# Down projections of three feed-forward layers: two narrow matmuls merged into one of 512 columns, eight PSUM banks in use, and the low halves added to x a chunk earlier

## The chip, the cores and the metric

The kernel runs on one core of a Trainium2 chip, as one program. The metric is the device time of one execution in microseconds (us). The median of three runs of the kernel before is 1074.24 us (1074.14 to 1075.94).

## The reference

Two transformer blocks over 256 tokens of width 1024, batch 1. The first has MoBA attention and differential attention, a cross attention to 256 memory tokens, a SwiGLU feed-forward layer and a final norm. The second is two layers deep: an attention and convolution mixer, then a gated linear attention mixer, each with a convolutional feed-forward layer and a per-layer embedding. Three parts of it hold the change, the down projections at the end of the three feed-forward layers. In the reference they are the last product of

```
def swiglu(x, norm_g, w_gate, w_up, w_down):
    h = rms_norm(x, norm_g)
    return (jax.nn.silu(h @ w_gate) * (h @ w_up)) @ w_down
...
        x = x + swiglu(x, ffn_norm_g[l], w_gate[l], w_up[l], w_down[l])
```

and the same in `_conv_ffn` of the second block, with a depthwise convolution and GELU ahead of it. The hidden width is 2816, the output width 1024, all in float32.

## The kernel before, in words

Activations lie features first: a tile has 128 features on the partitions and 256 tokens (T) in the free dimension; x has 8 such tiles (KT). A float32 product is made of three fp32r matmuls. Each operand is split into a high part (the fp32r rounding) and a low part (the rest): high weight times high activation, high weight times low activation, low weight times high activation, all summed in PSUM.

Weights come in chunks of 128 x 2048 (1 MB), one DMA each, through three slots (U) of `raw`. ScalarE (ACT) writes the high part of a chunk to `w_hi`, VectorE (DVE) the low part to `w_lo`, both two chunks ahead of the chunk that TensorE (PE) works on. These two steps are called `ahead(name, j, jm)` on either engine; on DVE it counts `lo_done` up. A load waits for `lo_done` of the chunk three before it; ACT's split of a chunk waits for `chunk_done`, that is for PE to be done with the slot. SP issues the loads.

The list `PHASES` gives the order of the 20 phases and their numbers of chunks. In an ordinary phase a chunk makes two output tiles (8 k-steps x 2 tiles x 3 matmuls) in one of three PSUM banks, the ring G; DVE or ACT evicts the bank and counts `evicted` up. The other five banks are D0 to D4; D4 is also called STAT and takes the sums of squares of the norms (`norm_sum`). Each layer's up phase has 22 chunks; an evicted chunk becomes one hidden tile, of which ACT writes the high part (`hidden_hi`) and DVE the low part (`hidden_lo`, counted by `hid_split`). The high parts of the 22 tiles lie in `hid_hi`, the low parts in `hid_lo`.

A down phase (down0, down1, down2) has 11 chunks, each with two input tiles and all 8 output tiles. `chunk_k` issues them: for both input tiles h and the 8 output tiles f, three matmuls of 256 columns. All 8 output tiles are summed in D0 to D3, two tiles to a bank, over all 11 chunks. Ten chunks go by input tile first; the eleventh by output tile first, so that tiles get done in order. When a pair of tiles is done, PE counts `full_dve` up (the last pair: `chunk_done`), and DVE's `down` adds the whole bank to two tiles of x (512 columns) and counts `x_ready`. ACT's `prep` and DVE's `prep_pair` then split the gained tiles into the high and low parts that the next phase needs, ACT also squares them; DVE's last split (`ahead`) of the stage stands behind these. `acquire` and `fill` keep, for each D bank, the semaphore and the count after which it is free.

After down0 comes hy_in; its first chunk waits for `x_split` at each k-step. After down1 and down2 comes a projection chunk (proj1, proj2, also by `chunk_k`), into D0 to D3, and four chunks of gate1 or gate2. The first of these calls `norm_sum` ahead of k-step 4.

The order of work on each engine is as the program is written; loops (`count.each`) peel three or four turns and run the rest in hardware loops of three turns. The change touches `chunk_k`, `ffn`, `embedding` and `chunk` on PE, `prep` and `hidden_hi` on ACT, `hidden_lo` and `down` on DVE. In the profile L499 is the helper `mm`, L918 ACT's helper `fn`, L1329, L1332 and L1335 DVE's `mul`, `add` and `sub`, L1339 `fused`.

Of the kernel before, what the change touches and what calls it, by code (L numbers as in the profile page):

```python
# [37 lines left out]
U = 3  # L38
# [24 lines left out]
for _name, _rows in PARAMS:  # L63
# [13 lines left out]
          ("up2", FT, 0), ("down2", FT // 2, 1), ("proj2", 1, 1), ("gate2", 4, 0)]  # L77
W_IN_Q = 6
# [59 lines left out]
def program(nc, io, out):  # L138
    with ExitStack() as stack:
# [164 lines left out]
        x_hi_done, x_split = sem("x_hi_done"), sem("x_split")  # L304
        sq_done, sq_total, sq_for_pe, att_squared = sem("sq_done"), sem("sq_total"), sem("sq_for_pe"), sem("att_squared")
# [174 lines left out]
        def _(pe):  # L480
            count = Counts(pe)
            due = {}
            free_at = {}
# [20 lines left out]
            def chunk(name, j, jm, moving, fresh=False, between=None, at_k=None):  # L504
# [69 lines left out]
            def chunk_k(name, j, jm, moving, k0):  # L574

                c, slot = j + FIRST[name], (FIRST[name] + jm) % U
                first = isinstance(j, int) and j == 0
                final = isinstance(j, int) and j == COUNT[name] - 1
                pe.wait_ge(lo_done, c + 1)

                order = [(h, f) for f in range(KT) for h in range(2)] if final else [(h, f) for h in range(2) for f in range(KT)]
                for h, f in order:
                    if first and h == 0 and f % 2 == 0:
                        acquire(f // 2)
                    to = D[f // 2][:, (f % 2) * T:(f % 2 + 1) * T]
                    cols = slice(h * DM + f * P, h * DM + (f + 1) * P)
                    m_hi, m_lo = (tile_at(m, k0 + h) for m in moving)
                    mm(to, w_hi[:, slot, cols], m_hi, first and h == 0 and f % 2 == 0, False)
                    mm(to, w_hi[:, slot, cols], m_lo, False, False)
                    last = mm(to, w_lo[:, slot, cols], m_hi, False, final and h == 1)  # L590
                    if final and h == 1 and f in (1, 3, 5) and name[:4] == "down":
                        fill(f // 2, last, full_dve, x_ready)
                last.then_inc(chunk_done, 1)
                if final and name[:4] == "down":
                    fill(3, None, None, x_ready)
# [158 lines left out]
            def ffn(layer, moving):  # L754
                outputs(f"up{layer}", moving)

                def body(j, jm):
                    pe.wait_ge(hid_split, count.next(hid_split, 2))
                    chunk_k(f"down{layer}", j, jm, (hid_hi, hid_lo), j * 2)
                count.each(COUNT[f"down{layer}"], body)  # L760
# [42 lines left out]
            def embedding(layer, moving):  # L803

                pe.wait_ge(p_split, count.next(p_split))
                chunk_k(f"proj{layer}", 0, 0, (p_hi, p_lo), 0)
# [106 lines left out]
        def _(act):  # L913
# [195 lines left out]
            def hidden_hi(j, jm, ring):  # L1109

                act.wait_ge(hid_done, count.next(hid_done))
                fn(tile_at(hid_hi, j), ring[:, jm % U, :]).then_inc(hid_hi_done, 1)
# [212 lines left out]
        def _(dve):  # L1325
# [290 lines left out]
            def hidden_lo(j, jm, ring):  # L1616
# [3 lines left out]
                sub(tile_at(hid_lo, j), ring[:, jm % U, :], tile_at(hid_hi, j).bitcast(F32)).then_inc(hid_split, 1)  # L1620

            def down(layer, moving, gain, g0=0, between=None, first=0):
# [574 lines left out]
```

## Time and profile before

| | us |
|---|---|
| median of 3 runs | 1074.24 (1074.14 to 1075.94) |
| the profiled execution | 1074.56 |
| its span | 1072.8 |
| TensorE busy in it | 1064.6 (99%) |
| VectorE busy | 819.5 (76%) |
| ScalarE busy | 645.5 (60%) |
| GpSimd busy | 2.7 |
| DMA | 187.00 MB, mean 174 GB/s |

The span is the time from the first to the last recorded instruction of the profiled execution; what lies around it is in the execution's time but not in the span. A busy time is the union over an engine's instructions; those of TensorE overlap one another, so the sum over its groups is larger than the busy time, and the mean duration of one is not what one costs in a row of many. The distance from one start to the next is.

### The profile page before, as it was taken

What the parts mean: (1) busy time and instruction counts of PE and PEld (TensorE: products, weight loads), DVE (VectorE), ACT (ScalarE), POOL (GpSimd) and SP (SyncE); (2) the same over time, 40 slices, a digit from 0 to 9 for tenths busy, and PEclk for the clock granted to TensorE, in tenths of its full rate; (3) what the DMA queues carried; (4) which work ended last, traced back from release to release, by engine and by line L of the source; (5) the groups of instructions that cost most, each with busy time, mean ns of one, the idle gap of its engine ahead of it and who ended that gap; (6) DMA issues with size and microseconds to landing.
All of it is one profiled execution on the core that took longest, in us unless ns stands there. A gap on an engine that the chain in (4) does not pass through costs nothing.

```text
span 1072.8 us, 21353 instructions
## 1 busy us (share of the span) xinstructions
PE 1064.6 (99%) x8496; PEld 1038.4 (97%) x8496; DVE 819.5 (76%) x1045; ACT 645.5 (60%) x898; POOL 2.7 (0%) x8
## 2 busy tenths in 40 slices
PE   9999999999999999999999999999999999999998
PEld 8989998999999999989999999999899999999998
DVE  6889877476666747898888895498988778888466
ACT  6667554455444436676787765475537587776453
POOL 0000000000000000000000000000000000000000
PEclk9999999999999999999999999999999999999999
DMA  9942553363454563544454556454432545445631
GB/s 346 255 157 79 181 213 123 113 245 131 185 189 167 195 227 142 174 152 158 158 196 170 192 191 226 172 181 158 157 118 79 196 158 195 171 191 197 227 135 71
DMA packets 30535, 187.00 MB, mean 174 GB/s; under 512 B 3735, under 2 KB 6520, under 8 KB 8840
## 3 DMA queue, kind: packets, MB, share of 16 engines
q1 hardware_dynamic: 29896, 185.05, 48.4%
q10 hardware_dynamic: 576, 1.05, 0.3%
q8 instruction: 47, 0.77, 0.3%
q14 instruction: 16, 0.13, 0.0%
HBM read 183.96 MB, written 1.34 MB: 173 GB/s over the span
## 4 chain that ended last, share of the span: by engine, by line
PE 97%; DVE 2%; DMA 1%; ACT 0%; issue 0%; SPq 0%; DVEq 0%
PE g L499 71%; PE d L499 25%; PE d L502 1%; DMA raw<-weights 1%; DVE w_lo L1335 0%; DVE gla_w L1329 0%; DVE b_lo L1339 0%; DVE gla_v L1469 0%; DVE gla_z L1335 0%; ACT b_hi L918 0%; DVE gla_s L1989 0%; SPq L425 0%; ACT hy_probs_t L918 0%; DVE gla_e L1335 0%; ACT w_hi L918 0%
## 5 line engine op out<-in xcount | busy, mean ns | idle before, releaser
L1335 DVE TENSOR_TENSOR w_lo<-raw,w_hi 128x2048 fp32r<-128x2048 f32 (+1 forms) x174 | 388.9, 2237 | 77.1 <-ACT w_hi L918 76.5
L918 ACT ACTIVATE w_hi<-raw 128x2048 fp32r<-128x2048 f32 (+1 forms) x174 | 324.1, 1867 | 119.7 <-PE d L499 85.1
L499 PE MATMUL g<-a_hi,w_hi 128*128 128x256 f32 x1232 | 352.8, 286 | 1.4 <-DVE w_lo L1335 1.3
L499 PE MATMUL g<-a_lo,w_hi 128*128 128x256 f32 x1232 | 348.8, 283 | 0.0
L499 PE MATMUL g<-a_hi,w_lo 128*128 128x256 f32 x1232 | 348.8, 283 | 0.0
L499 PEld LDWEIGHTS g<-a_hi,w_hi 128*128 128x128 f32 x1232 | 236.5, 192 | 4.4 <-DVE w_lo L1335 3.0
L499 PEld LDWEIGHTS g<-a_lo,w_hi 128*128 128x128 f32 x1232 | 236.7, 192 | 0.3
L499 PEld LDWEIGHTS g<-a_hi,w_lo 128*128 128x128 f32 x1232 | 236.5, 192 | 0.0
L499 PE MATMUL g<-b_hi,w_hi 128*128 128x256 f32 x656 | 186.6, 284 | 0.8 <-DVE b_lo L1335 0.7
L499 PE MATMUL g<-b_lo,w_hi 128*128 128x256 f32 x656 | 185.6, 283 | 0.0
L499 PE MATMUL g<-b_hi,w_lo 128*128 128x256 f32 x656 | 185.6, 283 | 0.0
L499 PE MATMUL d<-hid_hi,w_hi 128*128 (+1 forms) x528 | 148.8, 282 | 0.0
L499 PE MATMUL d<-hid_hi,w_lo 128*128 (+1 forms) x528 | 148.6, 281 | 0.0
L499 PE MATMUL d<-hid_lo,w_hi 128*128 (+1 forms) x528 | 148.6, 281 | 0.0
L499 PEld LDWEIGHTS g<-b_hi,w_hi 128*128 128x128 f32 x656 | 125.9, 192 | 1.4 <-issue 0.9
L499 PEld LDWEIGHTS g<-b_lo,w_hi 128*128 128x128 f32 x656 | 125.9, 192 | 0.1
L499 PEld LDWEIGHTS g<-b_hi,w_lo 128*128 128x128 f32 x656 | 125.9, 192 | 0.0
L499 PEld LDWEIGHTS d<-hid_hi,w_hi 128*128 128x128 f32 x528 | 99.4, 188 | 0.0
L499 PEld LDWEIGHTS d<-hid_lo,w_hi 128*128 128x128 f32 x528 | 99.4, 188 | 0.0
L499 PEld LDWEIGHTS d<-hid_hi,w_lo 128*128 128x128 f32 x528 | 99.4, 188 | 0.0
L918 ACT ACTIVATE conv_out<-conv_in,par 128x256 f32<-128x256 f32 x88 | 48.1, 594 | 41.2 <-DVE conv_in L1329 41.2
L1329 DVE TENSOR_TENSOR conv_in<-g,rstd 128x512 f32<-128x512 f32 x44 | 30.4, 690 | 14.8 <-PE g L499 14.6
(304 smaller groups left out, 1252.2 us busy)
## 6 DMA issues: line engine op xcount, KB each, us to landing
raw<-weights SPq DMA_DIRECT2D x168, 1024.0 KB, 4.9
bias_tab<-bias_dram SPq DMA_DIRECT2D x8, 192.0 KB, 9.8
x<-x_t ACTq DMA_DIRECT2D x4, 256.0 KB, 5.4
raw<-weights SPq DMA_DIRECT2D x4, 256.0 KB, 6.1
raw<-weights SPq DMA_DIRECT2D x2, 512.0 KB, 7.4
mem_t<-mem_t SPq DMA_DIRECT2D x1, 1024.0 KB, 9.6
out<-x SPq DMA_DIRECT2D x3, 256.0 KB, 2.3
hy_swap<-hy_qk SPq DMA_DIRECT2D x4, 128.0 KB, 6.3
```

The costliest lines, as they stand in the source:

```text
L499: return pe.matmul(out, lhsT, rhs, start=start, stop=stop, skip_group_check=True)
L502: return pe.transpose(out, src, ident[0:n, 0:n])
L918: return act.activation(out, in_, func, **kw)
L1329: return dve.tensor_tensor(out, a, b, ALU.mult)
L1335: return dve.tensor_tensor(out, a, b, ALU.subtract)
```

## The change

`hid_hi` and `hid_lo` become one tensor `hid_both`, in which the high part and the low part of an input tile lie side by side (T columns each), so that both can be the moving operand of a single matmul of 512 columns. `project` is the old loop for the projections, by input tile in all cases. `down_chunk` issues the first nine chunks of a down phase: one matmul of 512 columns with the high weight and one of 256 with the low weight. Its output takes a whole bank for each output tile: the left half gets the products with the high part, the right half those of the high weight with the low part. The eight banks are D0 to D3, STAT and the three of the ring G (`down_place`); their first use waits for the evictions of the up phase's last chunks. `down_end` issues the tenth and eleventh chunk with three matmuls of 256 columns into the left half, output tile by output tile. On DVE, as each tile of the tenth chunk is done, the right half is added to x (`lo_added`), with the split of the coming chunk after the fourth; the tiles of the eleventh chunk then each add their left half. PE's eleventh chunk waits for `lo_added` before each tile. In the first gate chunk `norm_sum` goes from k-step 4 to 5.

```diff
-        hid_hi = at("hid_hi", H, [FT, T], F32R)
+        hid_both = at("hid_both", H, [FT * 2 * T], F32R)
-        hid_lo = at("hid_lo", H + 22 * KB, [FT, T], F32R)
...
+        def hid_at(part, j):
+
+            return hid_both[:, bass.ds(j * (2 * T) + part * T, T)]
+
+        def down_place(name, f):
+
+            if name == "down0":
+                held, ring = (None, None, None, STAT, 0, 1, 2, 3)[f], f
+            else:
+                held, ring = (0, 1, 2, 3, STAT, None, None, None)[f], f - 5
+            if held is not None:
+                return D[held], held, None
+            ring = (FIRST_OUT[AFTER_DOWN[name]] + ring) % U
+            return G[ring], None, ring
...
+                ring = (FIRST_OUT[name] + jm) % U
+                if ring in ring_free_at:
+                    pe.wait_ge(x_ready, ring_free_at.pop(ring))
...
+            def down_chunk(name, j, jm):
 
                 c, slot = j + FIRST[name], (FIRST[name] + jm) % U
+                opened = isinstance(j, int) and j == 0
+                pe.wait_ge(hid_split, count.next(hid_split, 2))
                 pe.wait_ge(lo_done, c + 1)
+                for h in range(2):
+                    for i in range(KT):
+                        f = (i + 3) % KT if name == "down0" else i
+                        to, bank, ring = down_place(name, f)
+                        if opened and h == 0:
+                            if bank is None:
+                                pe.wait_ge(evicted, FIRST_OUT[AFTER_DOWN[name]] - U + (i - 5) + 1)
+                            else:
+                                acquire(bank)
+                        cols = slice(h * DM + f * P, h * DM + (f + 1) * P)
+                        both = hid_both[:, bass.ds(j * (4 * T) + h * 2 * T, 2 * T)]
+                        mm(to[:], w_hi[:, slot, cols], both, opened and h == 0, False)
+                        last = mm(to[:, 0:T], w_lo[:, slot, cols], hid_at(0, j * 2 + h), False, False)
                 last.then_inc(chunk_done, 1)
+
+            def down_end(name):
+
+                for j in (COUNT[name] - 2, COUNT[name] - 1):
+                    c, final = FIRST[name] + j, j == COUNT[name] - 1
+                    pe.wait_ge(hid_split, count.next(hid_split, 2))
+                    pe.wait_ge(lo_done, c + 1)
+                    for f in range(KT):
+                        to, bank, ring = down_place(name, f)
+                        if final:
+                            pe.wait_ge(lo_added, count.next(lo_added))
+                        for h in range(2):
+                            cols = slice(h * DM + f * P, h * DM + (f + 1) * P)
+                            mm(to[:, 0:T], w_hi[:, c % U, cols], hid_at(0, j * 2 + h), False, False)
+                            mm(to[:, 0:T], w_hi[:, c % U, cols], hid_at(1, j * 2 + h), False, False)
+                            last = mm(to[:, 0:T], w_lo[:, c % U, cols], hid_at(0, j * 2 + h), False, final and h == 1)
+                        if f < KT - 1:
+                            last.then_inc(full_dve, 1)
+                        else:
+                            last.then_inc(chunk_done, 1)
...
-                    chunk(f"gate{layer}", j, j % U, moving, fresh=j == 0, between=norm_sum, at_k=4 if j == 0 else None)
+                    chunk(f"gate{layer}", j, j % U, moving, fresh=j == 0, between=norm_sum, at_k=5 if j == 0 else None)
...
-                    act.wait_ge(ready, count.next(ready))
+                    act.wait_ge(ready, count.next(ready, 2))
...
-                count.each(COUNT[name] - first - 1, body)
-                for b in range(4):
-                    if b < 3:
+                count.each(COUNT[name] - first - 2, body)
+
+                def wait_for(f, chunk):
+                    if f < KT - 1:
                         dve.wait_ge(full_dve, count.next(full_dve))
                     else:
-                        dve.wait_ge(chunk_done, FIRST[name] + COUNT[name])
-                    pair = x[:, 2 * b:2 * b + 2, :]
-                    add(pair, pair, as_tiles(D[b][:])).then_inc(x_ready, count.one(x_ready))
-                    if b > 0:
-                        prep_pair(moving, gain, g0, x, b - 1)
+                        dve.wait_ge(chunk_done, FIRST[name] + chunk + 1)
+                    return x[:, f, :], down_place(name, f)[0]
+
+                for f in range(KT):
+                    tile, bank = wait_for(f, COUNT[name] - 2)
+                    add(tile, tile, bank[:, T:2 * T]).then_inc(lo_added, count.one(lo_added))
+                    if f == 3:
+                        ahead(name, COUNT[name] - 2, (COUNT[name] - 2) % U)
+                dve.wait_ge(lo_added, count.sent[lo_added])
+                for f in range(KT):
+                    tile, bank = wait_for(f, COUNT[name] - 1)
+                    add(tile, tile, bank[:, 0:T]).then_inc(x_ready, count.one(x_ready))
+                    if f % 2 == 1 and f > 1:
+                        prep_pair(moving, gain, g0, x, f // 2 - 1)
                 dve.wait_ge(x_ready, count.sent[x_ready])
                 prep_pair(moving, gain, g0, x, 3)
                 ahead(name, COUNT[name] - 1, (COUNT[name] - 1) % U)
```

## Rows read from the trace of the kernel before

**Rows 1.** The page: busy time per engine; granted TensorE clock in 40 slices, tenths.
```profile
PE 1064.6 (99%) x8496; PEld 1038.4 (97%) x8496; DVE 819.5 (76%) x1045; ACT 645.5 (60%) x898; POOL 2.7 (0%) x8
...
PEclk9999999999999999999999999999999999999999
```

**Rows 2.** Chain that ended last, 340 to 420 us: start, length, what.
```profile
349.92 4.32 PE g L499 x36
354.24 62.66 PE d L499 x528
416.90 3.11 PE g L499 x26
```

**Rows 3.** Windows, TensorE, second and third down stage: length, busy (matmuls), clock, DMA share, GB/s.
```profile
634.20:696.70 62.50, 62.50 (x528) 1.00 0.56 202
976.60:1039.10 62.50, 62.50 (x528) 1.00 0.55 202
```

**Rows 4.** Timeline of TensorE, matmuls of 512 columns: start, duration, engine, line.
```profile
175.72 0.39 PE L499 MATMUL g<-w_lo,b_hi 128*128 128x512 f32 x1
...
177.99 0.39 PE L499 MATMUL g<-w_hi,b_lo 128*128 128x512 f32 x1
```

**Rows 5.** Groups by line and shape: count, busy us in sum, mean ns, idle before.
```profile
L499 PE MATMUL d<-hid_hi,w_hi 128*128 128x256 f32 x240 | 67.7, 282 | 0.0
...
L499 PEld LDWEIGHTS d<-hid_hi,w_hi 128*128 128x128 f32 x528 | 99.4, 188 | 0.0
```

**Rows 6.** Timeline of DVE as the first and second down stages begin.
```profile
354.28 0.42 DVE L1329 TENSOR_TENSOR gate_z<-g,rstd 128x256 f32<-128x256 f32 x1 [1.82 <-PE g L499]
354.62 0.41 DVE L1329 TENSOR_TENSOR up_z<-g,rstd 128x256 f32<-128x256 f32 x1
...
634.24 0.69 DVE L1329 TENSOR_TENSOR conv_in<-g,rstd 128x512 f32<-128x512 f32 x1 [0.34 <-PE g L499]
```

**Rows 7.** Timeline of DVE in the second down stage, splits of its fourth and fifth chunk.
```profile
647.71 4.49 DVE L1335 TENSOR_TENSOR w_lo<-raw,w_hi 128x2048 fp32r<-128x2048 f32 x2 [1.11 <-ACT w_hi L918]
```

**Rows 8.** Timeline of DVE at the end of the first down stage.
```profile
407.55 2.29 DVE L1335 TENSOR_TENSOR w_lo<-raw,w_hi 128x2048 fp32r<-128x2048 f32 x1 [3.46 <-ACT w_hi L918]
412.67 0.69 DVE L1332 TENSOR_TENSOR x<-x,d 128x512 f32<-128x512 f32 x1 [2.82 <-PE d L499]
...
414.70 0.87 DVE L1339 SCALAR_TENSOR_TENSOR a_lo<-x,both_g,a_hi 128x256 fp32r<-128x256 f32 x2
...
416.94 0.69 DVE L1332 TENSOR_TENSOR x<-x,d 128x512 f32<-128x512 f32 x1
417.54 1.67 DVE L1339 SCALAR_TENSOR_TENSOR a_lo<-x,both_g,a_hi 128x256 fp32r<-128x256 f32 x4
419.12 2.28 DVE L1335 TENSOR_TENSOR w_lo<-raw,w_hi 128x2048 fp32r<-128x2048 f32 x1
```

**Rows 9.** Timeline of ACT at the end of the first down stage.
```profile
405.61 1.91 ACT L918 ACTIVATE w_hi<-raw 128x2048 fp32r<-128x2048 f32 x1 [3.84 <-PE d L499]
411.30 1.92 ACT L918 ACTIVATE w_hi<-raw 128x2048 fp32r<-128x2048 f32 x1 [3.78 <-PE d L499]
```

**Rows 10.** The page, DMA issues: tile, count, KB, median us to landing.
```profile
raw<-weights SPq DMA_DIRECT2D x168, 1024.0 KB, 4.9
```

**Rows 11.** Timeline of DVE at the first gate chunk of gate1.
```profile
704.08 2.28 DVE L1335 TENSOR_TENSOR w_lo<-raw,w_hi 128x2048 fp32r<-128x2048 f32 x1
706.28 0.42 DVE L1376 TENSOR_SCALAR mean_sq<-d 128x256 f32<-128x256 f32 x1
...
708.11 0.43 DVE L1339 SCALAR_TENSOR_TENSOR rstd<-newton,rough 128x256 f32<-128x256 f32 x1
708.97 0.69 DVE L1329 TENSOR_TENSOR ple_z<-g,rstd 128x512 f32<-128x512 f32 x1 [0.44 <-PE g L499]
```

More of the change, by code:

```diff
@@ L77 @@
           ("up2", FT, 0), ("down2", FT // 2, 1), ("proj2", 1, 1), ("gate2", 4, 0)]
+AFTER_DOWN = {"down0": "hy_in", "down1": "gate1", "down2": "gate2"}
 W_IN_Q = 6
@@ L304, in program @@
         x_hi_done, x_split = sem("x_hi_done"), sem("x_split")
+        lo_added = sem("lo_added")
         sq_done, sq_total, sq_for_pe, att_squared = sem("sq_done"), sem("sq_total"), sem("sq_for_pe"), sem("att_squared")
@@ L482, in _ @@
             due = {}
-            free_at = {}
+            free_at, ring_free_at = {}, {}
             def acquire(b):
@@ L572, in turn_scale, with project @@
                 fill(STAT, last, full_dve, drained_dve)
-            def chunk_k(name, j, jm, moving, k0):
+            def project(name, moving):
+                c = FIRST[name]
+                pe.wait_ge(lo_done, c + 1)
+                for h in range(2):
+                    for f in range(KT):
+                        if h == 0 and f % 2 == 0:
+                            acquire(f // 2)
+                        to = D[f // 2][:, (f % 2) * T:(f % 2 + 1) * T]
+                        cols = slice(h * DM + f * P, h * DM + (f + 1) * P)
+                        mm(to, w_hi[:, c % U, cols], moving[0][:, h, :], h == 0 and f % 2 == 0, False)
+                        mm(to, w_hi[:, c % U, cols], moving[1][:, h, :], False, False)
+                        last = mm(to, w_lo[:, c % U, cols], moving[0][:, h, :], False, h == 1)
+                last.then_inc(chunk_done, 1)
@@ L576, in chunk_k @@
+            def down_chunk(name, j, jm):
                 c, slot = j + FIRST[name], (FIRST[name] + jm) % U
-                first = isinstance(j, int) and j == 0
-                final = isinstance(j, int) and j == COUNT[name] - 1
+                opened = isinstance(j, int) and j == 0
+                pe.wait_ge(hid_split, count.next(hid_split, 2))
                 pe.wait_ge(lo_done, c + 1)
-                order = [(h, f) for f in range(KT) for h in range(2)] if final else [(h, f) for h in range(2) for f in range(KT)]
@@ L582, in chunk_k @@
[L582 to L592, printed above, removed]
@@ new lines, in down_chunk @@
+                last.then_inc(chunk_done, 1)
+            def down_end(name):
+                for j in (COUNT[name] - 2, COUNT[name] - 1):
+                    c, final = FIRST[name] + j, j == COUNT[name] - 1
+                    pe.wait_ge(hid_split, count.next(hid_split, 2))
+                    pe.wait_ge(lo_done, c + 1)
+                    for f in range(KT):
+                        to, bank, ring = down_place(name, f)
+                        if final:
+                            pe.wait_ge(lo_added, count.next(lo_added))
+                        for h in range(2):
+                            cols = slice(h * DM + f * P, h * DM + (f + 1) * P)
+                            mm(to[:, 0:T], w_hi[:, c % U, cols], hid_at(0, j * 2 + h), False, False)
[4 more added lines that the diff above has]
+                        else:
+                            last.then_inc(chunk_done, 1)
+                        if final:
+                            due[x_ready] = due.get(x_ready, 0) + 1
+                            if bank is None:
+                                ring_free_at[ring] = due[x_ready]
+                            else:
+                                free_at[bank] = (x_ready, due[x_ready])
@@ L755, in ffn @@
                 outputs(f"up{layer}", moving)
[L757 to L760, printed above, removed]
+                name = f"down{layer}"
+                count.each(COUNT[name] - 2, lambda j, jm: down_chunk(name, j, jm))
+                down_end(name)
             ffn(0, B)
@@ L1111, in hidden_hi @@
                 act.wait_ge(hid_done, count.next(hid_done))
-                fn(tile_at(hid_hi, j), ring[:, jm % U, :]).then_inc(hid_hi_done, 1)
+                fn(hid_at(0, j), ring[:, jm % U, :]).then_inc(hid_hi_done, 1)
             def down(layer, first=0, between=None):
@@ L1619, in hidden_lo @@
                 dve.wait_ge(hid_done, count.sent[hid_done])
-                sub(tile_at(hid_lo, j), ring[:, jm % U, :], tile_at(hid_hi, j).bitcast(F32)).then_inc(hid_split, 1)
+                sub(hid_at(1, j), ring[:, jm % U, :], hid_at(0, j).bitcast(F32)).then_inc(hid_split, 1)
             def down(layer, moving, gain, g0=0, between=None, first=0):
@@ L1629, in body @@
                         between(j)
-                count.each(COUNT[name] - first - 1, body)
-                for b in range(4):
-                    if b < 3:
+                count.each(COUNT[name] - first - 2, body)
+                def wait_for(f, chunk):
+                    if f < KT - 1:
                         dve.wait_ge(full_dve, count.next(full_dve))
                     else:
-                        dve.wait_ge(chunk_done, FIRST[name] + COUNT[name])
-                    pair = x[:, 2 * b:2 * b + 2, :]
-                    add(pair, pair, as_tiles(D[b][:])).then_inc(x_ready, count.one(x_ready))
-                    if b > 0:
-                        prep_pair(moving, gain, g0, x, b - 1)
+                        dve.wait_ge(chunk_done, FIRST[name] + chunk + 1)
[6 more added lines that the diff above has]
+                dve.wait_ge(lo_added, count.sent[lo_added])
+                for f in range(KT):
+                    tile, bank = wait_for(f, COUNT[name] - 1)
+                    add(tile, tile, bank[:, 0:T]).then_inc(x_ready, count.one(x_ready))
+                    if f % 2 == 1 and f > 1:
+                        prep_pair(moving, gain, g0, x, f // 2 - 1)
                 dve.wait_ge(x_ready, count.sent[x_ready])
```

4 lines of the change are left out of this document (1 added, 3 removed).

## The prediction, made before the changed kernel had been timed

> **What bounds the kernel now.** I read the page's busy shares and slices first. TensorE (PE) is busy 1064.6 of 1072.8 us, at full granted clock (2.4 GHz) in all 40 slices; VectorE (DVE) at 76% and ScalarE (ACT) at 60% have room [rows 1]. The reader is to see that one engine has no idle time to give back. Second, the chain of waits around the first of the three down stages: one unbroken piece of PE work, 528 matmuls in 62.66 us, with PE pieces on both sides [rows 2]. The two later down stages take 62.5 us each for 528 [rows 3]. So a down stage costs what its matmuls cost at their spacing, and only that spacing or a new wait can move the time. The grouped durations (281 ns for a 256-column matmul [rows 5]) mislead here, since matmuls overlap; the spacing is 62.66 / 528 = 118.7 ns.
>
> **The spacing of a wide matmul.** The kernel before already has fp32r matmuls of 512 columns, in the chunks that produce values by tokens. In the order of time, from 175.72 to 177.99 us lie 10 spacings: 227 ns each [rows 4]. A 256-column matmul on the normalised activations is spaced 4.32 / 36 = 120 ns [rows 2]. So 256 more columns add 107 ns, which is 256 columns at 2.4 GHz (106.7 ns), and about 13 ns per matmul do not grow with the width. On the hidden tiles the 256-column spacing is 118.7 ns, so that part is 12 ns. The weight load (188 ns long, beside a matmul of 281 [rows 5]) keeps pace with the 118.7 ns now and has 227 ns in which to do it afterwards, so it doesn't set the new spacing.
> The Trainium skill ("TensorE: Matmul & The Clock Gate", section "Back-to-back issue gap") gives N/2.4 + 2.5 ns for an isolated stream. By that rule one matmul fewer per pair would save only 2.5 ns, and the change would be worth an estimated 1.1 us in all. The rows above show some 12 ns instead, so I don't use it, but it is the rule that speaks against the change. The same section's sustained figure, 131 ns for 512 columns with their weight load, would save over 40 us; the 227 ns contradict it as well.
>
> **Part 1: pairs merged, nine chunks of each stage.** Per chunk there are 16 places (8 output tiles times 2 input tiles). Each had three 256-column matmuls: high weight on high part, high weight on low part, low weight on high part. Now the first two are one of 512 columns. That is 3 stages x 9 chunks x 16 = 432 pairs. A pair cost 2 x 118.7 = 237.3 ns. The wide one costs between 225.7 (118.7 + 107) and 227 ns [rows 2, 4]. Saved per pair: 10.3 to 11.6 ns, so 4.5 to 5.0 us; I take 226.3 ns, the middle, hence 11.0 ns and 4.75 us. The nearest rows are a direct measurement of the same width and type, though with the roles of weight and activation exchanged; the far ends for the unseen form are a wide matmul that costs two narrow ones (gain 0) and one with no fixed part (213.3 ns: 24 ns, 10.4 us).
>
> **Part 2: eight banks instead of four.** The first down chunk now opens three banks of the G ring, which the last up chunks have just filled. The waits stand at the sixth to eighth output tile of the first input tile, each tile costing 226.3 + 118.7 = 345 ns. The last one asks for the last up chunk's eviction 7 x 345 = 2.4 us after that chunk's end. In the first stage the eviction runs from 354.62 to 355.03, some 0.8 us after the stage began, and in the second it ends at 634.93, 0.7 us after [rows 6]. Cost 0, with 1.6 us of cover. If the DVE were in a weight split (2.29 us [rows 8]) at that moment, it would cost up to 0.7 us a stage.
>
> **Part 3: the tenth chunk.** It and the eleventh keep narrow matmuls (no gain, no loss), now tile by tile: a tile takes 6 x 118.7 = 0.71 us. DVE gets 8 low adds of 256 columns from PSUM, 0.41 us each (the up_z row has that shape [rows 6]), and in the eleventh chunk 8 adds of that size in place of 4 of 0.69 [rows 8]. In all 8 x 0.41 + 8 x 0.41 - 4 x 0.69 = 3.8 us more DVE work per stage. What hides it is DVE's idle time: 3.4 us before each split in these chunks [rows 8]. Counted from the tenth chunk's start: the fourth low add ends at about 3.5 us; the weight split behind it finds its high part ready at 2.1 us (ACT starts at the chunk's edge and takes 1.92 [rows 9]), and ends at 5.8; the low adds of tiles 5 to 8 end by 7.2. The eleventh chunk starts at 5.7 and asks for tile 5 at 5.7 + 4 x 0.71 = 8.5, when its add has been done since 6.2. Cover 2.3 us, cost 0. This split ends 1.4 us later than now and so releases a weight load that much later; a load lands in 4.9 us [rows 10] and its data are wanted more than 10 us later: 0.
>
> **Part 4: the end of the stage.** Before: last add at 416.94 (0.69), four a_lo tiles 1.67, then the split, over at 421.4, 4.5 us after the last down matmul [rows 8]. After: one add of 0.41, the same four tiles, the same split, so about 0.3 us earlier. DVE's work between the eleventh chunk's first and last tile is 7 x 0.41 + 4 x 0.42 = 4.6 us in 5.0, and it starts some 0.5 us late from the low adds, so it may still carry 0.1 to 0.3 us. That cancels. The next chunk wants this split's result 5.76 us after the end, so 1.2 us stays: cost 0. The next phase's first G bank holds the first tile drained (hy_in) or is asked for a whole projection chunk later (gate), so these waits are met too. ACT issues the same instructions as before. SP and POOL issue nothing new.
>
> **Part 5: the down chunks run faster than their weights are prepared.** The tightest split in the trace is that of the fourth chunk of the second stage: two splits from 647.71, over at 652.2, so its own at 649.95, wanted at 634.2 + 3 x 5.70 = 651.3 [rows 7]. After the change a chunk takes 16 x 345 = 5.52 us, so it is wanted at 650.8. Cover 0.8 us, cost 0. Weight traffic is 200 to 202 GB/s at 55% of the DMA engines [rows 3] and goes up by 3%.
>
> **Part 6: norm_sum one k-step later in the first gate chunk, projection in another order.** The mean at 706.28 starts when DVE leaves the split before it, rstd is done at 708.5 and the gate's eviction at 709.6 [rows 11]. Six matmuls later (0.72 us) shifts this by at most 0.7. The split behind it then ends at 712.6 instead of 711.9, and the third gate chunk wants it at about 696.7 + 5.7 + 2 x 5.76 = 713.9. Cost 0; if that cover of 1.3 us were gone, whatever exceeded it. The projection has the same 48 matmuls, and its banks are freed tile by tile from the eleventh chunk's start: 0.
>
> **Sum.** The profiled execution took 1074.56 us, 1.76 more than its span of 1072.8. The change takes 4.75 from the span: 1068.05, or 1069.8 for such an execution. The median of the runs is 0.32 below the profiled one, so 1069.5.
>
> **Rivals.**
> A. The fixed part per matmul doesn't go away with the merged one: with hidden tiles as the moving operand a matmul of 512 columns costs nearly two narrow ones, 232.3 to 237.3 ns. For it: no row has activations moving at that width, and 118.7 against 120 ns show that the operand matters. Against it: by 1.3 ns only, and the wide rows lie at 227. Time: 432 x 0 to 5 ns, so 1072.1 to 1074.24, no change that shows. Chance 0.05. (The Trainium skill's isolated spacing, cited above, would put the time into this rival's range.)
> B. The gain is there but PE waits somewhere in each stage. The thinnest cover is Part 5's 0.8 us, then the 1.2 of Part 4. If these failed by 1 us in each stage, 3 us are lost: 1072.5, faster by less than 0.2%. Chance 0.07.
> C. Slower: DVE falls behind at the tenth chunk. The split between the low adds waits for ACT's high part, hence for a weight load; all of tiles 5 to 8 stand behind it, and PE's eleventh chunk behind them. It decides from 2.3 us of lateness, and the kernel is slower only when the three stages lose more than 4.75 together, so with a split late by 2.3 + 1.6 = 3.9 us in each. With 3 us lost per stage: 1074.24 - 4.75 + 9 = 1078.5. Against it: loads land in 4.9 us and ACT sits idle 3.8 us waiting for PE, not for DMA [rows 9, 10]. Chance 0.04.
> D. More gain: whatever takes 1.3 ns off a narrow matmul with hidden tiles (118.7 against 120) takes about 5 off a wide one, so 222 ns: 15.3 ns x 432 = 6.6 us, 1067.6. No row speaks for or against it. Chance 0.08.
> The forecast itself: 0.76, with 1069.1 to 1070.2 as its own range.
>
> **Numbers.** A measurement of this kernel can tell about 0.2%, 2.15 us, from no change. The forecast and D are faster by more than that (0.84), B in part (0.04): faster 0.88. A and the rest of B: same 0.08. C: slower 0.04. The range for 8 in 10 reaches to D below and into B above: 1067.8 to 1071.6.
>
> **What would show it.** Down stages of about 1.6 us less each (61.1 us); the wide matmuls spaced 226 to 227 ns; no PE spacing above 350 ns at the sixth to eighth tile of a first down chunk, at a tile of the eleventh chunk, or at the fourth chunk of the second stage; the split after the last add over before the next chunk asks for it. The prediction is wrong if the wide spacing is outside 225 to 228 ns, or if PE waits for lo_added, evicted or lo_done in these places.

## The result and the profile after

The changed kernel takes 1076.09 us (median of 20 runs, 1074.64 to 1078.10), the kernel before 1074.65 in 20 runs beside it. The ratio is 1.0013 (95% interval 1.0008 to 1.0019): 1.4 us slower, below the 0.2% that the prediction called no change. Predicted were 1069.5 us and a range from 1067.8 to 1071.6.

The page of the changed kernel, busy times and groups (the last columns are busy us, mean ns, idle before):

```profile
PE 1065.9 (99%) x8064; PEld 1018.9 (95%) x8064; DVE 829.8 (77%) x1081; ACT 645.6 (60%) x898; POOL 2.7 (0%) x8
...
PEclk9999999999999999999999999999999999999999
...
L515 PE MATMUL d<-hid_both,w_hi 128*128 (+2 forms) x390 | 119.2, 360 | 0.0
```

There are 432 matmuls fewer than in [rows 1], and the busy time is 1.3 us longer. The busy share says nothing here: waits of under 0.2 us lie inside it, and so does time at the lower clock. Nor does the row of clock digits, in which a 9 stands for 90% or more: the kernel before, which the prediction read as at full clock in all 40 slices, has a stretch at half the clock too (window, length, busy, clock, DMA share, GB/s):

```profile
796.80:800.10 3.30, 3.30 (x17) 0.50 0.00 0
```

What tells is the spacing of starts and the length of each stretch. The chain, one piece of 528 matmuls in [rows 2], is now cut into pieces of 10 and 6, since the output goes to D and G banks in turn:

```profile
351.91 3.72 PE g L515 x31
355.63 1.74 PE d L515 x10
357.37 1.05 PE g L515 x6
358.42 1.76 PE d L515 x10
```

A timeline of TensorE in down0:

```profile
361.77 0.40 PE L515 MATMUL d<-hid_both,w_hi 128*128 128x512 f32 x1
362.01 0.28 PE L515 MATMUL d<-hid_both,w_lo 128*128 128x256 f32 x1
362.13 0.39 PE L515 MATMUL d<-hid_both,w_hi 128*128 128x512 f32 x1
362.35 0.28 PE L515 MATMUL d<-hid_both,w_lo 128*128 128x256 f32 x1
362.47 0.40 PE L515 MATMUL d<-hid_both,w_hi 128*128 128x512 f32 x1
362.71 0.28 PE L515 MATMUL d<-hid_both,w_lo 128*128 128x256 f32 x1
362.83 0.40 PE L515 MATMUL g<-hid_both,w_hi 128*128 128x512 f32 x1
```

These are three places in 1.06 us. A place is one wide matmul and the narrow one behind it. The wide one is spaced 224 to 235 ns (mean of all 144: 230.5), the narrow one 120.5. A place costs 351.0 ns, against 356 before and 345 forecast.

To see where the time went, I took the starts of the first matmul of each stretch from the traces and their differences, in us. "to up1" is hy_in and hy_out, "to up2" is proj1, gate1, gla_in and gla_out; the first column is the start of down0.

| kernel | start | down0 | to up1 | up1 | down1 | to up2 | up2 | down2 |
|---|---|---|---|---|---|---|---|---|
| before | 354.08 | 62.66 | 89.59 | 127.71 | 62.79 | 152.66 | 127.13 | 62.73 |
| before, again | 354.33 | 62.66 | 89.59 | 127.71 | 62.78 | 152.63 | 127.15 | 62.73 |
| changed | 355.46 | 62.07 | 90.64 | 128.44 | 62.34 | 151.20 | 128.31 | 62.39 |
| changed, 2nd | 354.95 | 62.07 | 90.62 | 128.45 | 62.21 | 151.09 | 128.28 | 62.39 |
| changed, 3rd | 354.33 | 62.07 | 89.59 | 128.47 | 62.21 | 152.61 | 128.30 | 62.25 |

The down stages and the up stages repeat to 0.2 us. The down stages give back 1.4 to 1.6 us in sum, where 4.75 were forecast. up1 and up2, which the prediction left out, lose 0.7 and 1.2 us: 1.9 us. Three columns jump between executions of the changed kernel: "to up1" by 1.0 us, "to up2" by 1.5 and the start by 1.1. The first two jumps are explained below, with c1, c2 and c4.

VectorE in up1, first of the kernel before:

```profile
570.53 0.69 DVE L1329 TENSOR_TENSOR conv_in<-g,rstd 128x512 f32<-128x512 f32 x1 [0.34 <-PE g L499]
571.14 0.41 DVE L1329 TENSOR_TENSOR conv_hid<-conv_gelu,conv_out 128x256 f32<-128x256 f32 x1
571.79 0.43 DVE L1335 TENSOR_TENSOR hid_lo<-conv_hid,hid_hi 128x256 f32 x1 [0.24 <-DVE conv_hid L1329]
...
573.65 2.28 DVE L1335 TENSOR_TENSOR w_lo<-raw,w_hi 128x2048 fp32r<-128x2048 f32 x1
```

and of the changed one:

```profile
572.63 0.69 DVE L1386 TENSOR_TENSOR conv_in<-g,rstd 128x512 f32<-128x512 f32 x1 [0.43 <-PE g L515]
573.24 0.41 DVE L1386 TENSOR_TENSOR conv_hid<-conv_gelu,conv_out 128x256 f32<-128x256 f32 x1
573.98 0.43 DVE L1392 TENSOR_TENSOR hid_both<-conv_hid,hid_both 128x256 f32 x1 [0.33 <-DVE conv_hid L1386]
...
575.84 2.29 DVE L1392 TENSOR_TENSOR w_lo<-raw,w_hi 128x2048 fp32r<-128x2048 f32 x1
```

From the eviction's start to the split's start it was 3.12 us and is 3.21. The 0.09 stand in the brackets, 0.33 for 0.24 (in up2 0.26 for 0.17): VectorE waits for its own product of a hidden tile and then works out the address of the low part. The trace's records of VectorE's sequencer, which these views leave out, have one FUSED_REGOPS between that wait and the low part in the kernel before, and a FUSED_REGOPS and one ALU_OP in the changed one.

TensorE where a chunk of up1 begins, first in the kernel before:

```profile
570.21 0.28 PE L499 MATMUL g<-a_hi,w_lo 128*128 128x256 f32 x1
570.33 0.37 PE L499 MATMUL g<-a_hi,w_hi 128*128 128x256 f32 x1
570.54 0.28 PE L499 MATMUL g<-a_lo,w_hi 128*128 128x256 f32 x1
```

and in the changed one:

```profile
578.06 0.28 PE L515 MATMUL g<-a_hi,w_lo 128*128 128x256 f32 x1
578.26 0.38 PE L515 MATMUL g<-a_hi,w_hi 128*128 128x256 f32 x1
578.48 0.28 PE L515 MATMUL g<-a_lo,w_hi 128*128 128x256 f32 x1
```

The spacings are 0.12 and 0.21 us before, 0.20 and 0.22 in the changed kernel, where 0.12 is a spacing without a wait. Both come again at every second chunk, before from about 559 to 605 us and in the changed kernel from about 543 to 625. So up1 of the kernel before had small waits already. Its splits end 0.14 us ahead of every second chunk of up1 and 0.21 ahead of those of up2; where TensorE waits in the changed kernel that distance is about 0.13. There was thus next to no cover in up1 and about 0.08 us in up2, and the change takes 0.09.

### The profile page after: what moved, and what is told of

It is laid out like the page before. It is cut to its first block, busy times and chain, and to the rows that moved or that the text cites. A ratio compares the mean times of both kernels' runs of the same rounds, so it can differ in the third digit from the quotient of the medians.

```text
span 1074.3 us, 20551 instructions
## 1 busy us (share of the span) xinstructions
PE 1065.9 (99%) x8064; PEld 1018.9 (95%) x8064; DVE 829.8 (77%) x1081; ACT 645.6 (60%) x898; POOL 2.7 (0%) x8
## 3 DMA queue, kind: packets, MB, share of 16 engines
q10 hardware_dynamic: 576, 1.05, 0.3%
## 4 chain that ended last, share of the span: by engine, by line
PE 92%; DVE 4%; DMA 3%; ACT 1%; issue 0%; SPq 0%; DVEq 0%; ACTq 0%
PE g L515 73%; PE d L515 18%; DMA raw<-weights 3%; DVE w_lo L1392 2%; PE d L518 1%; ACT w_hi L975 1%; DVE gla_w L1386 0%; DVE scores L1396 0%; DVE row_max L1479 0%; DVE qkv L1386 0%; DVE b_lo L1396 0%; DVE gla_v L1526 0%; DVE gla_z L1392 0%; DVE gla_s L2056 0%; DVE a_lo L1396 0%
## 5 line engine op out<-in xcount | busy, mean ns | idle before, releaser
L515 PEld LDWEIGHTS g<-a_hi,w_hi 128*128 128x128 f32 x1232 | 236.7, 192 | 6.7 <-DVE w_lo L1392 3.3
L515 PE MATMUL d<-hid_both,w_hi 128*128 (+2 forms) x390 | 119.2, 360 | 0.0
L515 PE MATMUL d<-hid_both,w_lo 128*128 (+1 forms) x330 | 93.4, 283 | 0.0
L515 PEld LDWEIGHTS d<-hid_both,w_hi 128*128 128x128 f32 x390 | 69.3, 188 | 12.2 <-issue 0.6
L515 PE MATMUL g<-hid_both,w_hi 128*128 (+2 forms) x234 | 72.3, 359 | 0.0
L515 PEld LDWEIGHTS d<-hid_both,w_lo 128*128 128x128 f32 x330 | 62.1, 188 | 0.0
L515 PE MATMUL g<-hid_both,w_lo 128*128 (+1 forms) x198 | 56.1, 283 | 0.0
L515 PEld LDWEIGHTS g<-hid_both,w_hi 128*128 128x128 f32 x234 | 41.6, 188 | 7.1
```

The source lines that it names most:

```text
L515: return pe.matmul(out, lhsT, rhs, start=start, stop=stop, skip_group_check=True)
```

## The experiments

The theory after the first comparison had two parts. R: the new layout costs a register instruction in VectorE's loops, which lengthens a chain that had no cover. S: the merged matmuls do gain, but less than forecast. Times are medians; each is given with its ratio to the kernel before in runs beside it (1074.2 to 1074.5 us). The ratio is the one on record with its interval and can differ from the ratio of the two medians. The self wait is VectorE's wait for its own `hid_done` ahead of the low part.

**e1_layout_only**, on the kernel before:

```diff
-                sub(tile_at(hid_lo, j), ring[:, jm % U, :], tile_at(hid_hi, j).bitcast(F32))
+                sub(hid_at(1, j), ring[:, jm % U, :], hid_at(0, j).bitcast(F32))
```

with `hid_both` and `hid_at` of the change, its addresses on TensorE and ScalarE too, and all matmuls narrow.

> The kernel before with only the layout of the change: high and low parts of a hidden tile side by side in one tensor, all matmuls as before. Theory R (registers): the low part's address in a hardware loop now needs one register instruction more on VectorE, which stands between the product of a hidden tile and its low part; the idle time ahead of that instruction goes from 0.24 to 0.33 us in up1 and up2, the split of the chunk to come ends 0.09 us later per chunk, and TensorE waits 50 to 80 ns at every second chunk of up1 and up2: 0.5 to 1.5 us slower than before, up0 unchanged. Rival L (the layout matters only to TensorE's reading): the idle time stays 0.24, up1 and up2 keep their length, and the narrow spacing in the down stages goes from 118.7 to 120 ns: +0.7 us per stage.

1078.12 us, ratio 1.0036 (1.0023 to 1.0048). up1 128.87, up2 127.86 us: 1.16 and 0.73 longer than before, 1.9 us, above the 0.5 to 1.5 expected. The profile has two stretches at the lower clock besides (below), so the median is not a measure of the 1.9. down0 62.66 with 118.7 ns spacing, so rival L fell: the layout does nothing to narrow matmuls.

**e8_register_only**, the sharper form: all tiles where they were, only the expression changed. TensorE's `chunk_k` reads the low tile by the same expression; that loop runs in the down stages and projections, not in the up stages.

```diff
-        hid_lo = at("hid_lo", H + 22 * KB, [FT, T], F32R)
+        hid_lo = at("hid_lo", H + 21 * KB, [FT + 1, T], F32R)
...
-                sub(tile_at(hid_lo, j), ring[:, jm % U, :], ...)
+                sub(flat(hid_lo)[:, bass.ds(j * T + T, T)], ring[:, jm % U, :], ...)
```

> The kernel before, all tiles at their old addresses; only the low part's tile is addressed by an expression of its own (tile number plus one, in a tensor that begins one tile earlier), which gives VectorE in its hardware loops as many register instructions more as the layout of the change does. Theory R: idle time ahead of the low part 0.33 instead of 0.24 us, TensorE waits at every second chunk of up1 and up2, about 2 us slower than before, as e1_layout_only without its clock stretches. Rival: what cost the time in e1_layout_only was where the tiles lie; this one is equal to before within 0.5 us.

1077.59 us, ratio 1.0019 (1.0008 to 1.0029): 2.0 us by the ratio, 3.3 by the two medians. up1 is 128.87 and up2 127.84 us: to 0.02 us those of e1. down0 keeps its 62.66 us. VectorE's bracket has the 0.33, and the sequencer's records have the ALU_OP:

```profile
568.80 0.42 DVE L1335 TENSOR_TENSOR hid_lo<-conv_hid,hid_hi 128x256 f32 x1 [0.33 <-DVE conv_hid L1329]
```

So R is shown, and the rival (the place of the tiles) fell: an address expression alone costs 1.9 us in these two stretches. The changed kernel loses the same sum in other shares (0.7 and 1.2 us for 1.16 and 0.7); why they differ is not shown.

**e4_no_self_wait**, on the changed kernel:

```diff
                 dve.wait_ge(hid_hi_done, count.next(hid_hi_done))
-                dve.wait_ge(hid_done, count.sent[hid_done])
```

> The changed kernel without VectorE's wait for its own hid_done ahead of the low part of an older hidden tile (the tile it reads is covered by the wait for ScalarE's high part). Theory R: the idle time of 0.33 us ahead of the low part is gone, the weight split of each chunk of up1 and up2 ends about 0.3 us earlier, TensorE's waits of 50 to 120 ns at every second chunk there and at the second chunk of down1 vanish: 1 to 2 us faster than changed. Rival: these waits come from late weight loads (the split starts by the landing, not by VectorE's chain) and stay; equal within 0.5 us.

1071.73 us, ratio 0.9974 (0.9965 to 0.9983). up1 and up2 are 127.14 us, all three down stages 62.07. The bracket is gone:

```profile
569.63 0.69 DVE L1386 TENSOR_TENSOR conv_in<-g,rstd 128x512 f32<-128x512 f32 x1 [0.68 <-PE g L515]
570.24 0.42 DVE L1386 TENSOR_TENSOR conv_hid<-conv_gelu,conv_out 128x256 f32<-128x256 f32 x1
570.57 0.42 DVE L1392 TENSOR_TENSOR hid_both<-conv_hid,hid_both 128x256 f32 x1
```

VectorE now waits 0.68 us for TensorE, where it had 0.25 to 0.43: this is the cover that was missing. The wait was for the newest hidden tile, while the tile that is read is one older and covered by ScalarE's count. The register instructions now run while VectorE still works on earlier instructions, where the wait had kept them behind the product. The splits end 0.48 us ahead of their chunk in place of 0.13, so the cover is 0.35 us.

The gain on the changed kernel is 4.2 us by the ratios, above the 1 to 2 expected. The traces show 3.1 of it: 1.3 in up1, 1.2 in up2 and 0.6 in down1 and down2. A part of the rest may be the clock: none of the eight profiles without the self wait has the stretch at 1.2 GHz in gla_in, six of the nine with it have. Why is not shown.

**e5_before_no_wait** and **c3_before_no_wait_again**, the same line taken out of the kernel before.

> The kernel before without VectorE's wait for its own hid_done ahead of the low part. Theory R2 (before, the chain of VectorE in up1 and up2 just fitted: its split ended 0.14 us ahead of the chunk, and what the change lost there was that cover): nothing waits in these phases before, so little comes of it: 0 to 0.6 us faster than before, up1 and up2 at 126.5 to 127 us as they are. Rival: the self wait cost the kernel before as much as the changed one, 3 to 4 us faster.

> The kernel before without the self wait, once more: its profiled execution showed no stretch at 1.2 GHz behind the first ones, while its runs scatter over 3 us. If the scatter is made of such stretches, this one may show one of 1.4 us, at 445 or at 798 us; up1 and up2 stay as in e5_before_no_wait.

1073.57 us, ratio 0.9997 (0.9985 to 1.0009); the single time of c3 is 1074.44, and its profile has a stretch at the lower clock from 446 us, where e5's has none. up1 goes from 127.71 to 127.14, up2 from 127.13 to 127.14. The kernel before had 0.6 us to gain there at most, the changed one 2.5: the expected time holds, and the rival (as much in both) falls. That nothing waits in these stretches was right for up2 and not for up1. The pair e5 and e4 shows the change without its side effect. The down stages go from 62.66 us to 62.07, the stretches between them stay within 0.1 us, and the spans of the two profiles, neither of which has a stretch at the lower clock, go from 1070.6 to 1068.8 us. So the same change gains 1.8 us once the self wait is out of both.

**e2_narrow**, on the changed kernel:

```diff
-                        mm(to[:], w_hi[:, slot, cols], both, opened and h == 0, False)
+                        mm(to[:, 0:T], w_hi[:, slot, cols], hid_at(0, j * 2 + h), opened and h == 0, False)
+                        mm(to[:, T:2 * T], w_hi[:, slot, cols], hid_at(1, j * 2 + h), False, False)
```

> The changed kernel with each 512-column matmul taken apart into two of 256 columns into the same two halves of the bank; all else as changed. Theory S (spacing): a place of the nine chunks costs 230.5 + 120.3 = 350.8 ns in the changed kernel, and three narrow ones cost 356 to 360, so this kernel is 2.2 to 4.0 us slower than the changed one and slower than before by 3 to 5 us, since the losses elsewhere stay. Rival N: the wide matmul gives nothing (the nine chunks of a stage keep their length), the two are equal within 0.5 us.

1076.68 us, ratio 1.0022 (1.0012 to 1.0031). The narrow spacing is 118.7 ns as before the change and down0 62.66 us, so the wide matmuls gain 0.59 us in down0 (0.5 in down1 and down2, where both kernels have waits), and rival N fell. By medians it is only 0.6 us above the changed kernel, by the ratios 1.0, where 2.2 to 4.0 were expected: that range missed. It took 360 ns for a place at its upper end, and at both ends it left out that narrow matmuls throughout make the tenth and eleventh chunk 0.12 us a stage shorter. The difference of two medians is blurred besides by the stretches at the lower clock: e2's profile has them at both places.

**e3_shifted**, **e7_shift_no_wait**, **e10_shift_64**, **e11_shift_512**: the hidden tiles' region moved, by 128 bytes in e3 and e7, 64 in e10, 512 in e11. The last three are without the self wait.

```diff
-        H = place["at"]
+        H = place["at"] + 128
```

> The changed kernel with the region of the hidden tiles moved by 128 bytes, so that hidden tiles start at the same offset within 1 KB as weights and the other activations. Theory A (the place of the moving operand in SBUF sets the spacing): the wide spacing, now in turns of 224, 234 and 234 ns, becomes an even 227 as in the token chunks, the narrow 120; a place 347 ns, 1.7 us less than changed in the three stages. Rival O (it is the pairing of a wide and a narrow matmul, or the operand's role): the spacings stay 224/234/234 and 120, no change of time.

> The changed kernel without the self wait, and with the hidden tiles' region moved by 128 bytes. Both gains should add up if they are of different kinds: down0 62.4, down1 and down2 61.0 us (in e3_shifted 61.8 with 0.8 us of waits in them), so 1.7 us faster than e4_no_self_wait. Rival: the shorter down1 and down2 of e3_shifted came with its waits and are 62.1 without them; equal to e4_no_self_wait.

> The changed kernel without the self wait, the hidden tiles' region moved by 64 bytes. Theory A2 (the tiles' offset sets the spacing, and 128 bytes was only the wrong one): other spacings again than 230.5 and 120.3, as 236.7 and 118.0 at 128 bytes; a stage between 61.3 and 62.4 us. Rival: only the step of 128 bytes matters, 64 leaves 62.07 us a stage.

> The changed kernel without the self wait, the hidden tiles' region moved by 512 bytes. Theory A2: spacings of their own, 61.3 to 62.4 us a stage. Rival: a wide matmul of 2 KB meets the same pieces of memory at any multiple of its parts, 230.5 and 120.3 as unshifted, 62.07 us.

Medians 1074.38 us (ratio 1.0002, 0.9993 to 1.0010), 1073.74 (1.0001, 0.9988 to 1.0014), and one time each for the last two, 1070.86 and 1070.51. The spacings in down0:

| moved by | wide, ns | narrow beside it, ns | last two chunks, ns | stage, us |
|---|---|---|---|---|
| 0 (e4) | 230.5 | 120.5 | 120.0 | 62.07 |
| 128 (e3, e7) | 236.7 | 116.7 | 120.0 | 62.40 |
| 64 (e10) | 235.0 | 118.3 | 117.8 | 62.18 |
| 512 (e11) | 230.5 | 120.5 | 120.0 | 62.07 |

Place does matter, by steps below 512 bytes, but no offset gave 227. Theory A in its first form fell, and so did rival O; A2 held for 64 bytes, its rival for 512.

In e3 down1 and down2, which have a short wait at the first and second chunk, ran at 231.5 and 115 ns from the third chunk on (61.8 us), and down0 at 236.7 and 116.7. In e7, without the waits, all three stages took 62.40 us: its expectation of 61.0 missed and its rival held. The changed kernel shows the like by itself: the tenth and eleventh chunk are spaced 120.0 ns in six of its nine profiled stages and 118.7 in three. So the same instructions on the same addresses have more than one steady spacing, and by e3 and e7 waits ahead can decide which. No run shows the mechanism.

**e6_wide_first** and **e9_tile_by_tile**, orders of a down chunk without the self wait. e6:

```diff
                         mm(to[:], w_hi[:, slot, cols], both, opened and h == 0, False)
+                    for f in range(KT):
+                        to, bank, ring = down_place(name, f)
+                        cols = slice(h * DM + f * P, h * DM + (f + 1) * P)
                         last = mm(to[:, 0:T], w_lo[:, slot, cols], hid_at(0, j * 2 + h), False, False)
```

e9 exchanges the loops over h and i.

> The changed kernel without the self wait, and with the order of a down chunk changed: for an input tile all 8 matmuls of 512 columns first, then the 8 of 256. Theory P (wide and narrow in turns disturb each other's spacing: 230.5 + 120.3 instead of 227 + 118.7): now in rows of their own they are spaced 227 and 118.7, a stage takes 61.3 instead of 62.07 us, 2 us faster than e4_no_self_wait. Rival Q (a wide matmul with hidden tiles as the moving operand costs 230.5 in any order): spacing 230 to 231 in the row of eight as well; within 0.5 us of e4_no_self_wait.

> The changed kernel without the self wait, the nine chunks output tile by output tile: both input tiles' matmuls (wide, narrow, wide, narrow) follow one another in the same bank. Theory B (the wide spacing of 230.5 comes from a change of bank after every pair; in the token chunks 12 matmuls of 512 columns follow one another in one bank, at 227): wide 227 to 229, a stage 61.6 to 61.8 us, 1 us faster than e4_no_self_wait. Rival: the order does nothing, 62.07 us a stage.

e6: 1071.30 us, ratio 0.9969 (0.9960 to 0.9979); wide 232.7 ns in rows of eight (227 to 241), narrow 118.5, a stage 61.95. Rival Q held in the main: the wide spacing does not fall to 227 without the turn of wide and narrow. e9: 1071.99 us, ratio 0.9977 (0.9967 to 0.9988), 62.07 us a stage: the change of bank does nothing, and theory B fell. e6 has the lowest median of the kernels with several runs, 3.2 us below the kernel before, but its interval overlaps e4's.

**c1_changed_again**, **c2_before_again**, **c4_changed_third**: repeats, for the table above.

> The changed kernel once more, to see which parts of its profile repeat. Steady (a property of the program): waits in up1 (0.7 us more than before), up2 (1.2 us), stages of 62.07, 62.34 and 62.39 us. Not steady (depends on the execution): the stretch at 1.2 GHz from 445.8 to 448.8 us, worth 1.4 us, and the 1.4 us lost by 60 us.

> The kernel before once more, to see which parts of its profile repeat: up1 and up2 with waits of 20 ns, stages of 62.66 to 62.8 us (steady), and whether the stretch at 1.2 GHz at 798 us comes again and one at 445 us comes here too (not steady).

> The changed kernel a third time. Steady by the two profiles so far: up1 128.44, up2 128.3, down stages 62.07, 62.3, 62.39 us, 151.1 us from down1 to up2. Open: whether the stretch at 1.2 GHz near 445 us (seen in both, and in 7 of 13 profiles of all kernels) comes again, 90.63 or 89.59 us from down0 to up1, and where the start of down0 lies (354.0 to 355.5).

1075.33, 1074.78 and 1075.13 us. Windows of the third execution of the changed kernel (columns as in [rows 3]):

```profile
444.50:448.20 3.70, 3.70 (x33) 1.00 0.38 84
797.40:800.30 2.90, 2.90 (x15) 0.50 0.00 0
```

and of the first, all engines (PE, PEld, DVE, ACT and POOL busy, then clock, DMA share, GB/s):

```profile
445.30:449.00 3.70, 3.70 (x21) 3.70 (x20) 3.67 (x4) 3.70 (x7) 0.00 (x0) 0.56 0.39 84
```

In the first execution TensorE fell to 1.2 GHz around 447 us (15 matmuls spaced 213 ns in place of 120, 1.4 us; net 1.05 in the column "to up1", since the longest spacing ahead of hy_out is 0.3 us then and 0.9 otherwise), in the third near 799 us. What TensorE did before each: matmuls of 2 to 8 columns and transposes in hy_in, matmuls of 64 columns with a wait of 0.8 us in gla_in. Of 17 profiles of all kernels 8 had the stretch in hy_in and 6 the one in gla_in. The changed kernel's three differ in both, the two of e5_before_no_wait's program in the first. Both executions of the kernel before have the one in gla_in.

## Why the prediction was wrong

- **Part 1, the wide spacing, failed in its size.** The mechanism was right (e2: merging gains 0.59 us in down0), but a place costs 351.0 ns and not 345. The wide one takes 230.5 and not 226.3, the narrow one beside it 120.5 and not 118.7. Over 432 places that is 2.6 of the 3.4 us by which the down stages miss the forecast. The text named the gap: no row of before had hidden tiles moving at that width. It then went by the nearest row and made its range 1.3 ns wide for an operand that already differed by 1.3 ns at half the width. The spacings of the other offsets, 230 to 237 ns, show what the bound should have been.
- **Part 3 failed in a small term.** "No gain, no loss" for the tenth and eleventh chunk: in down0 they kept the 120 ns of the chunks ahead, 5.76 in place of 5.70 us each. Of nine profiled stages six did so (up to 0.4 us an execution), and three had the 118.7 that was forecast. The work itself went as worked out. The changed kernel's VectorE has the fourth low add at 409.10, the split to 411.7, the last tile's adds in time and no wait of TensorE. The rows that answer to [rows 8]:

```profile
409.10 0.42 DVE L1389 TENSOR_TENSOR x<-x,d 128x256 f32<-128x256 f32 x1 [0.30 <-PE d L515]
409.43 2.28 DVE L1392 TENSOR_TENSOR w_lo<-raw,w_hi 128x2048 fp32r<-128x2048 f32 x1
...
418.10 1.67 DVE L1396 SCALAR_TENSOR_TENSOR a_lo<-x,both_g,a_hi 128x256 fp32r<-128x256 f32 x4
419.68 2.29 DVE L1392 TENSOR_TENSOR w_lo<-raw,w_hi 128x2048 fp32r<-128x2048 f32 x1
```

- **Parts 2, 4 and 6 held.** There is no spacing above 240 ns at a first use of a G bank in down0. The last split ends 4.4 us after the stage (4.5 before). proj1, gate1 and what follows to up2 are no longer than before, like compared with like: 152.61 us for 152.66 with the stretch at the lower clock.
- **Part 5 took the wrong chunk.** The tightest split is the second chunk's, not the fourth's. It stands behind the up phase's last eviction on VectorE. The trace of before had it already: the split ended at 639.65 us, 0.15 us ahead of the chunk, where the fourth chunk's had 1.3:

```profile
639.65 0.28 PE L499 MATMUL d<-hid_hi,w_lo 128*128 128x256 f32 x1
639.80 0.36 PE L499 MATMUL d<-hid_hi,w_hi 128*128 128x256 f32 x1
639.99 0.28 PE L499 MATMUL d<-hid_lo,w_hi 128*128 128x256 f32 x1
```

  In the changed kernel it ends at 642.27 us, when TensorE wants it:

```profile
642.18 0.28 PE L515 MATMUL g<-hid_both,w_lo 128*128 128x256 f32 x1
642.42 0.47 PE L515 MATMUL d<-hid_both,w_hi 128*128 128x512 f32 x1
642.73 0.28 PE L515 MATMUL d<-hid_both,w_lo 128*128 128x256 f32 x1
```

  The waits at the first and second chunk come to about 0.3 us in each of down1 and down2, where the kernel before has 0.1, and are gone in e4. They cost 0.4 us more than before in the two stages together.
- **A step was missing: the layout's cost outside the down stages.** The parts followed the matmuls; the same diff rewrites the address in `hidden_lo`, which runs in the loops of up1 and up2. There TensorE's next weights came 0.14 us ahead of their chunk in up1 and 0.21 in up2, of which 0.13 is no cover, and e8 shows that the one expression costs 1.9 us. up0 has 1.7 us of idle time on VectorE per chunk and lost nothing. This took more than the 1.5 us gained. The sum put these stretches at nothing without looking at them; without this term the steady parts would be 1.5 us faster than before.
- Rival B came closest in kind (a gain, and waits that eat it), at places it didn't name. Rival A's spacing (232 and more) was nearly met, C and D not.
- **What stays open.** The steady parts sum to 1.9 - 1.5 = 0.4 us slower; measured are 1.4 (0.9 to 2.0). The rest must lie in the parts that jump: the first 354 us and the two stretches at 1.2 GHz. Three profiles against two can't settle whether the change makes them likelier, but every run has a mean granted clock. It is below 0.998 in 9 of the changed kernel's 22 runs and in 14 of 75 of the kernel before (runs beside the experiments; the 20 beside the result have none on record). That points to more such stretches with the change and doesn't prove it, since the runs are of different sessions. Among runs at 0.998 the medians are 1075.27 and 1074.34 us, so 0.9 us remain, of which 0.4 are explained. Nor is it shown why a wide matmul takes 230 to 237 ns with hidden tiles and 227 in the token chunks.

## What to carry to other kernels

When TensorE bounds a kernel, look for the engine that feeds it with the least cover, in every stage that the diff's helpers run in, and measure the cover by the end of the last feeding instruction against the first matmul that wants it, less what this distance is where that matmul waits (0.13 us here). A layout that needs one more address expression in a hardware loop is not free where an engine's chain fills the period. Merging two matmuls saves what the spacing shows for that operand and place, some 5 ns a pair here and not 11. A good first thing to take out of a tight chain is a wait for one's own newest result where an older one is read and another wait covers it (2.5 us in up1 and up2 of the changed kernel, whose ratio went from 1.0013 to 0.9974).

## What the runs showed of the hardware that was not expected

- One register instruction more between a self wait and the VectorE instruction behind it costs 0.09 us each time (idle 0.33 for 0.24 us in up1, 0.26 for 0.17 in up2). Without the wait it costs nothing there (up1 is 127.14 us in e4 with it and in e5 without).
- From the end of a VectorE split to the start of a TensorE matmul that waits for it pass 0.13 us (up1 and up2 of the changed kernel).
- Spacing of fp32r matmuls at 2.4 GHz, steady within a stage: 256 columns 118.7 or 120 ns; 512 columns 227 (weights moving) or 230.5 to 236.7 (hidden tiles moving), changed by moving the tiles 64 or 128 bytes and not by 512.
- An identical stage in one program (e3) is at 236.7 and 116.7 ns in down0 and at 231.5 and 115 ns in down1, where the only difference seen is a short wait at its first and second chunk.
- Stretches of about 3 us at 1.2 GHz (granted clock 0.50 from 797.40 to 800.30 us in the third execution) come in a kernel whose TensorE is 99% busy, in some executions of a program and not in others: 8 of 17 profiles in hy_in, 6 of 17 in gla_in.
